# Experts' up stage: GpSimd's remainder pair placed ahead of its fetches, and the second token tile met by the weights' remainder at 128 columns

## The chip, the core and the metric

One Trainium2 chip, one of its cores. The metric is the device time of one launch in microseconds; lower is better. The kernel before took 3091.02 us (median of three runs, 3085.73 to 3091.17).

## What is computed

Two transformer blocks on 256 tokens of width 2048, in float32. The part that matters here is the last stage of the second block, the expert layer (`peer_ffn`). There are 16384 experts; each token chooses 128 of them (8 heads, 16 each) with gates.

```python
def block(args):
    xb, ib, gb = args
    u = expert_down[ib]
    act = jax.nn.gelu(jnp.einsum('tkd,td->tk', u, xb).astype(f32))
    vv = expert_up[ib]
    return jnp.einsum('tk,tkd->td', (gb * act).astype(vv.dtype), vv)
```

The kernel computes it densely for tokens 0 to 191: the activations of all 16384 experts (stage "peer_down"), multiplied with a gate matrix that is zero where an expert was not chosen, and then one dense product with `expert_up` (stage "peer_up", called the up stage here). For tokens 192 to 255 (`QT` = 64 of them) it fetches only the chosen rows of `expert_up` by indirect DMA and VectorE adds them up.

## The kernel before

**Exact products from rounded operands.** TensorE multiplies in the format fp32r. To keep float32 accuracy each operand is split into a rounded part (`hi` for weights, `h` for activations) and a remainder (`lo`, `l`), and three products are summed: rounded with rounded, remainder of the activations with rounded weights, rounded activations with the remainder of the weights.

**Pieces and rounds.** All weights come as one stream of pieces of 128 x 1024 elements, 512 KB each; four pieces are a round. In the up stage (`UPS` = 64 rounds; `UP0` is the number of rounds before it) every engine has its own hand-written program order:

- SyncE (`up_load`, L570) loads a piece into one of eight raw buffers once the remainder of the piece that lay there two rounds before is made (`lo_done`).
- ScalarE (`up_hi`, L1284) rounds piece k of round r into `hi[:, k]` once TensorE is through with piece k of the round before (L1288). For pieces 1 and 3 it also copies the raw piece into two banks of PSUM (`raw_copy`, L1301). Once a round it rounds the activations of the round after next into `hg` (`hidden_hi`, L1266).
- GpSimd makes the remainder of piece 0 of each round, in two halves of 512 columns (`up_lo`, L630, two instructions on L636, called the pair here). It also issues the indirect DMAs: the activations of chosen experts (`fetch_act`, L640, 64 in all, in rounds 1 to 26, five in each of rounds 1 and 2 and two or three after that) and the rows of `expert_up` (`fetch_row`, L646, 128 in all, two or three a round for rounds 3 to 30 and 33 to 62; a fetch moves 512 KB). A row goes into one of five buffers and waits until VectorE has added the row that lay there (L649).
- VectorE makes the remainders of pieces 1, 2 and 3 (`up_lo`, L2296; piece 2 from SBUF, 1 and 3 from the copies in PSUM), adds the fetched rows (`add_row`, L2312), and makes the remainder of the activations (`hidden_lo`, L2249, lines L2253 and L2255; both of its inputs are in SBUF). One round of it is: piece 1, row, piece 2, row, piece 3, perhaps a third row, activations.
- TensorE (`up_piece`, L3013) does per piece and per half of 512 columns five products into two PSUM banks, `a` for tokens 0 to 127 and `b` for tokens 128 to 191. The half's first three use the rounded weights (L3037 to L3039); the other two (L3041, L3042) need the remainder and wait for it (`ready`, L3040). 64 rounds x 4 pieces x 2 halves x 5 are 2560 products; in the last piece of each half of the stage the five stand in another order (L3030, L3031, L2390 to L2392).

**The stationary operands.** `hg` holds, for each slot and piece, 384 columns: remainder of tokens 0 to 127, rounded part of tokens 0 to 127, rounded part of tokens 128 to 191 (64 columns, `h_b`), remainder of tokens 128 to 191 (64 columns). `hl_b` is the last 128 columns, both parts of tokens 128 to 191 beside each other. So L3039 loads 128 columns and writes 128 partitions of `b`, the rounded part's product in the first 64 and the remainder's in the last 64; `add_residual` (L2338) adds the two halves at the end (L2342, L2343). L3041 loads the 64 columns of `h_b` alone and adds into the first 64 partitions.

**Order on GpSimd.** The pair of round 0 stands first. Then come three waits: for the table of rows (`slots_ready`), for the stores of the activations to DRAM (`side_stored`, L657 and L658) and for the end of the stage before (L659). After that the loop of L660 issues in round r the fetches of activations for r, the fetches of rows for r + 1, and then the pair of round r.

Of the kernel before, what the change touches and what calls it, by code (L numbers as in the profile page):

```python
# [29 lines left out]
P = 128  # L30
# [15 lines left out]
NT = 192  # L46
QT = T - NT
# [67 lines left out]
def build(nc, stream, cols, cons, band, dil, x, rpb, w_gates, gains, p_t, w_gd, up_fb,  # L115
          qk_gain, qk_cols, sub_keys, spill, side_acts, out):
    ctx = ExitStack()
    with ctx:
# [7 lines left out]
        def place(name, shape, at, dt=F32):  # L126
            return nc.alloc_sbuf_tensor_at(name, shape, dt, offset=base + at)
# [283 lines left out]
        hg = place("hg", [P, 2, 4, 3 * P], F_AT, F32R)  # L411
# [18 lines left out]
        def raw_up(r, k):  # L430
            return raws[(4 * r + k) % 8]

        def lo_up(k):
            return lo[:, k, :] if k < 2 else lo_x[:, k - 2, :]

        UP0 = ROUND0["peer_up"]
        UPS = 64
# [10 lines left out]
        def acts_at(r):  # L448

            if r < 3:  # L450
                return range(5 * (r - 1), 5 * r)
            return range(10 + (r - 3) * 54 // 24, 10 + (r - 2) * 54 // 24) if r < 27 else range(0)
# [156 lines left out]
        def _(pool):  # L609
# [20 lines left out]
            def up_lo(r):  # L630

                pool.wait_ge(hi_done, (UP0 + r) * 4 + 1)
                for half, used in enumerate((half_used, unit_used)):
                    pool.wait_ge(used, (UP0 + r) * 4 - (3 if r else 1))
                    n = slice(half * NCH, (half + 1) * NCH)
                    nc.gpsimd.tensor_tensor(lo_up(0)[:, n], raw_up(r, 0)[:, n],  # L636
                                            hi[:, 0, n].bitcast(F32), ALU.subtract)\
                        .then_inc(lo_done[0], 1)

            def fetch_act(q):  # L640
                nc.gpsimd.indirect_dma_start(
                    act_q[:, q:q + 1], None, side_acts.rearrange("i j (t a) -> (i j t) a", a=1),
                    bass.IndirectOffsetOnAxis(ap=row_act[:, q:q + 1], axis=0))\
                    .then_inc(got_act[q // 8], 16)
# [8 lines left out]
                    .then_inc(got_row[b], 16)  # L653

            up_lo(0)
            pool.wait_ge(slots_ready, 1)
            for g in range(4):  # L657
                pool.wait_ge(side_stored[g], 16 * 8)  # L658
            pool.wait_ge(unit_used, after("peer_up", 0))  # L659
            for r in range(1, UPS):  # L660
                for q in acts_at(r):
                    fetch_act(q)
                for n in rows_at(r + 1):
                    fetch_row(n)
                up_lo(r)


        @block.scalar
# [1716 lines left out]
        def _(pe):  # L2385
            M = nc.tensor
# [7 lines left out]
            def ready(i, k, half):  # L2394
                pe.wait_ge(lo_done[k], i * 2 + (half + 1))

            def rounded(i, k):
                pe.wait_ge(hi_done, i * 4 + (k + 1))
# [380 lines left out]
            for kb in range(KB):  # L2779
                ins = exact(ps[0:32, 4, 0:T], [m[:, kb, :] for m in (wgd_h, wgd_l)],  # L2780
                            [m[:, kb, :] for m in (xh, xl)], T, kb == 0, kb == KB - 1)
# [199 lines left out]
            for k in range(3):  # L2981
                for tt in range(TT):
                    ins = M.transpose(ps[:, 4 + k, tt * P:(tt + 1) * P],
                                      route[:, k, tt * P:(tt + 1) * P], ident)
# [28 lines left out]
            def up_piece(r, slot, k, half, first=False, last=False):  # L3013

                if k == 0:
                    pe.wait_ge(hl_done, r + 1)
                rounded(r + UP0, k)
                l_a, h_a, h_b, hl_b = (hg[:, slot, k, f] for f in (
                    slice(0, P), slice(P, 2 * P), slice(2 * P, P + NT), slice(2 * P, 3 * P)))
                for n in range(2):  # L3020
                    if first and half == 0:
                        pe.wait_ge(down_summed, 127 + n)
                    elif first and n == 0:
                        pe.wait_ge(acc_read, 1)
                    f = slice(n * NCH, (n + 1) * NCH)
                    w_h, w_l = hi[:, k, f], lo_up(k)[:, f]
                    a, b = (ps[:, 4 * half + 2 * tt + n, :] for tt in range(TT))
                    if last:
                        ready(r + UP0, k, n)
                        M.matmul(b[0:QT], h_b, w_l, start=False, stop=False)  # L3030
                        ins = M.matmul(b, hl_b, w_h, start=False, stop=True)  # L3031
                        if half:
                            ins.then_inc(bank_done, 1)
                        exact(a, (h_a, l_a), (w_h, w_l), NCH, False, True)\
                            .then_inc(bank_done if half else (half_used, unit_used)[n], 1)
                        continue
                    M.matmul(a, h_a, w_h, start=first, stop=False)  # L3037
                    M.matmul(a, l_a, w_h, start=False, stop=False)  # L3038
                    M.matmul(b, hl_b, w_h, start=first, stop=False)  # L3039
                    ready(r + UP0, k, n)  # L3040
                    M.matmul(b[0:QT], h_b, w_l, start=False, stop=False)  # L3041
                    M.matmul(a, h_a, w_l, start=False, stop=False)\  # L3042
                        .then_inc((half_used, unit_used)[n], 1)

# [137 lines left out]
```

## Time and profile before

| | us |
|---|---|
| median of three runs | 3091.02 |
| lowest and highest | 3085.73, 3091.17 |
| the profiled execution | 3095.82 |
| its span from first to last instruction | 3093.5 |
| up stage in it, start of first to start of last but one matmul | 2489.06 to 3087.23 |

| engine | busy us | share of the span |
|---|---|---|
| TensorE matmuls (PE) | 3069.1 | 99% |
| TensorE weight loads (PEld) | 2567.8 | 83% |
| VectorE (DVE) | 1654.9 | 53% |
| ScalarE (ACT) | 1671.4 | 54% |
| GpSimd (POOL) | 2533.4 | 82% |

All times in the profile are from one execution. Matmuls are pipelined, and the end of each is modelled, so the distance from one start to the next tells their pace, and the busy share does not. In the timeline a row has its start, its duration, engine and line, operation, destination and sources, shape and count, and in brackets the idle time before it with what ended it; "128*64" is the size of the stationary operand, 128 rows by 64 columns. "PEclk" is the granted clock of TensorE as a share of 2.4 GHz.

### The profile page before, as it was taken

How to read it: one execution, taken by the hardware profiler on the slowest of the kernel's cores; microseconds unless marked ns; L12 is line 12 of the kernel's file. 1: busy time of each engine (PE TensorE's matmuls, PEld its weight loads, DVE VectorE, ACT ScalarE, POOL GpSimd, SP SyncE). 2: the span in 40 equal slices, each digit the busy share in tenths (PEclk: the TensorE clock that was granted, in tenths of full speed). 3: DMA queues.
4: the chain of work that ended last, by engine and by line, in shares of the span. 5: the costliest groups of instructions: out<-in, count | busy, mean ns of one | idle time of the engine just before them, and what ended most of it. 6: DMA issues, size and time to landing. Idle time of an engine off the chain costs nothing.

```text
span 3093.5 us, 48732 instructions
## 1 busy us (share of the span) xinstructions
PE 3069.1 (99%) x15766; PEld 2567.8 (83%) x15766; DVE 1654.9 (53%) x2846; ACT 1671.4 (54%) x2515; POOL 2533.4 (82%) x1980
## 2 busy tenths in 40 slices
PE   9999999999999999999999999999999999999999
PEld 8888888888888887888888888888888877777777
DVE  5469244434410033655632357167772259998887
ACT  5754543433344455444544434477774467777776
POOL 7888989999999998797788889988889977765553
PEclk9999999999999999999999999999999999999999
DMA  6554655555565565454455655555555589999996
GB/s 237 174 169 152 195 177 184 185 187 183 183 204 194 193 201 176 146 187 164 145 164 189 203 184 189 193 180 175 181 178 195 195 316 355 350 345 355 350 362 239
DMA packets 188519, 659.88 MB, mean 213 GB/s; under 512 B 22864, under 2 KB 28112, under 8 KB 187888
## 3 DMA queue, kind: packets, MB, share of 16 engines
q1 hardware_dynamic: 159168, 573.64, 54.3%
q0 software_dynamic: 20480, 67.15, 6.1%
q10 hardware_dynamic: 8752, 17.60, 1.7%
q8 instruction: 62, 1.02, 0.1%
q14 instruction: 57, 0.47, 0.0%
HBM read 649.92 MB, written 8.39 MB: 213 GB/s over the span
## 4 chain that ended last, share of the span: by engine, by line
PE 94%; DVE 3%; POOL 1%; issue 1%; ACT 0%; DMA 0%; POOLq 0%; DVEq 0%; SPq 0%; ACTq 0%
PE ps L2401 30%; PE ps L2405 15%; PE ps L2499 8%; PE ps L2492 8%; PE ps L2494 8%; PE ps L3037 4%; PE ps L3041 4%; PE ps L3038 4%; PE ps L3042 4%; PE ps L3039 4%; PE ps L2557 3%; POOL lo L620 1%; PE ps L2552 0%; PE ps L2621 0%; DVE pos L2153 0%
## 5 line engine op out<-in xcount | busy, mean ns | idle before, releaser
L620 POOL TENSOR_TENSOR lo<-raw,hi 128x512 fp32r<-128x512 f32 x1656 | 2158.3, 1317 | 326.7 <-PE ps L2405 113.2
L2401 PE MATMUL ps<-xx,hi 128*128 128x512 f32 x4288 | 1521.9, 398 | 5.1 <-DVE xx L1333 5.1
L686 ACT ACTIVATE hi<-raw 128x1024 fp32r<-128x1024 f32 x827 | 869.1, 1059 | 841.6 <-PE ps L2405 432.7
L2405 PE MATMUL ps<-xx,lo 128*128 128x256 f32 x4288 | 1202.4, 280 | 1.7 <-POOL lo L620 1.7
L2401 PEld LDWEIGHTS ps<-xx,hi 128*128 128x128 f32 x4288 | 805.8, 188 | 191.3 <-DVE xx L1333 6.6
L2405 PEld LDWEIGHTS ps<-xx,lo 128*128 128x128 f32 x4288 | 810.4, 189 | 2.8 <-POOL lo L620 2.6
L2492 PE MATMUL ps<-hi,xx 128*128 128x512 f32 x608 | 241.1, 397 | 1.6 <-ACT hi L686 1.1
L2494 PE MATMUL ps<-hi,xx 128*128 128x512 f32 x608 | 237.0, 390 | 0.0
L650 POOL DMA_INDIRECT row<-in_stream,row_up x128 | 134.1, 1048 | 102.2 <-DVE ps L2321 80.9
L3037 PE MATMUL ps<-hi,hg 128*128 128x512 f32 x508 | 201.9, 397 | 0.6 <-issue 0.4
L3038 PE MATMUL ps<-hi,hg 128*128 128x512 f32 x508 | 199.6, 393 | 0.0
L3039 PE MATMUL ps<-hi,hg 128*128 128x512 f32 x508 | 197.7, 389 | 0.0
L2499 PE MATMUL ps<-lo,xx 128*128 128x512 f32 x608 | 188.8, 391 | 2.4 <-POOL lo L620 2.0
L1289 ACT ACTIVATE hi<-raw_up 128x1024 fp32r<-128x1024 f32 x128 | 135.0, 1056 | 80.0 <-PE ps L3042 67.1
L1289 ACT ACTIVATE hi<-raw 128x1024 fp32r<-128x1024 f32 x128 | 134.9, 1056 | 76.5 <-PE ps L3042 68.3
L1678 DVE TENSOR_TENSOR y<-ps,gbc 128x512 f32<-128x512 f32 x16 | 10.3, 686 | 285.2 <-ACT ps L934 285.2
L2321 DVE SCALAR_TENSOR_TENSOR ps<-row,coef,ps 128x1024 f32<-128x1024 f32 x126 | 160.9, 1277 | 0.0
L2229 DVE TENSOR_REDUCE ps<-ps 128x256 f32<-128x512 f32 x80 | 55.9, 699 | 161.2 <-PE ps L2405 161.2
L2499 PEld LDWEIGHTS ps<-lo,xx 128*128 128x128 f32 x608 | 113.3, 188 | 30.0 <-POOL lo L620 6.6
L2494 PE MATMUL ps<-hi,hid_l 128*128 128x512 f32 x352 | 136.9, 389 | 0.0
L2492 PE MATMUL ps<-hi,hid_h 128*128 128x512 f32 x352 | 136.9, 389 | 0.0
L2492 PEld LDWEIGHTS ps<-hi,xx 128*128 128x128 f32 x608 | 114.2, 188 | 27.3 <-issue 2.4
(393 smaller groups left out, 4394.7 us busy)
## 6 DMA issues: line engine op xcount, KB each, us to landing
raw<-in_stream SPq DMA_DIRECT2D x955, 512.0 KB, 3.3
raw_up<-in_stream SPq DMA_DIRECT2D x128, 512.0 KB
side_acts<-side ACTq DMA_DIRECT2D x32, 128.0 KB, 2.3
wg<-in_w_gates ACTq DMA_DIRECT2D x1, 2048.0 KB, 8.8
bias<-in_rpb ACTq DMA_DIRECT2D x1, 2048.0 KB, 8.0
gbc<-in_gains ACTq DMA_DIRECT2D x2, 1024.0 KB, 6.0
spill<-hx ACTq DMA_DIRECT2D x4, 512.0 KB, 3.8
row<-in_stream,row_up POOLq DMA_INDIRECT x128
```

What stands on the lines that cost most here:

```text
L620: nc.gpsimd.tensor_tensor(lo[:, k % 2, n], raw[:, k, n], hi[:, k, n].bitcast(F32), ALU.subtract)\
L686: nc.scalar.activation(hi[:, k, :], raw[:, k, :], ACT.Copy).then_inc(hi_done, 1)
L1289: nc.scalar.activation(hi[:, k, :], raw_up(r, k), ACT.Copy).then_inc(hi_done, 1)
L2321: V.scalar_tensor_tensor(out=accum(n), in0=rows_in[n % 5][:], scalar=c, in1=accum(n), op0=ALU.mult, op1=ALU.add).then_inc(row_used, 1)
L2401: M.matmul(ps[:, b_, :], w_h, xx[:, i_].rearrange("p a t -> p (a t)"), start=first, stop=False)
L2405: return M.matmul(t_bank(b_), w_l, xh[:, i_, :], start=False, stop=last)
L2492: M.matmul(ps[:, 2 * pair + tt, :], ah[:, kb0 + j, t], hi[:, k, f], start=first and j == 0, stop=False)
L2494: M.matmul(ps[:, 2 * pair + tt, :], al[:, kb0 + j, t], hi[:, k, f], start=False, stop=False)
L2499: return M.matmul(ps[:, 2 * pair + tt, :], ah[:, kb0 + j, t], lo[:, k % 2, f], start=False, stop=last and j == 1)
L3037: M.matmul(a, h_a, w_h, start=first, stop=False)
L3038: M.matmul(a, l_a, w_h, start=False, stop=False)
L3039: M.matmul(b, hl_b, w_h, start=first, stop=False)
```

## The change

Two edits. On GpSimd the pair of a round stands one place earlier: rounds 0 and 1 both come ahead of the three waits, and in round r the pair of r + 1 follows the fetches. On TensorE the product of the second token tile with the weights' remainder takes all 128 columns of `hl_b` instead of the 64 of `h_b`, so it also adds remainder times remainder into the last 64 partitions; in the last piece of a half the products with `w_h` and `w_l` change places.

```diff
             up_lo(0)
+            up_lo(1)
             pool.wait_ge(slots_ready, 1)
             for g in range(4):
                 pool.wait_ge(side_stored[g], 16 * 8)
...
                     fetch_act(q)
                 for n in rows_at(r + 1):
                     fetch_row(n)
-                up_lo(r)
+                if r + 1 < UPS:
+                    up_lo(r + 1)
...
-                l_a, h_a, h_b, hl_b = (hg[:, slot, k, f] for f in (
-                    slice(0, P), slice(P, 2 * P), slice(2 * P, P + NT), slice(2 * P, 3 * P)))
+                l_a, h_a, hl_b = (hg[:, slot, k, n * P:(n + 1) * P] for n in range(3))
...
                     if last:
                         ready(r + UP0, k, n)
-                        M.matmul(b[0:QT], h_b, w_l, start=False, stop=False)
-                        ins = M.matmul(b, hl_b, w_h, start=False, stop=True)
+                        M.matmul(b, hl_b, w_h, start=False, stop=False)
+                        ins = M.matmul(b, hl_b, w_l, start=False, stop=True)
...
                     ready(r + UP0, k, n)
-                    M.matmul(b[0:QT], h_b, w_l, start=False, stop=False)
+                    M.matmul(b, hl_b, w_l, start=False, stop=False)
```

## Rows read from the trace of the kernel before

**Rows 1.** The page: its span, and busy time by engine.
```profile
span 3093.5 us, 48732 instructions
...
PE 3069.1 (99%) x15766; PEld 2567.8 (83%) x15766; DVE 1654.9 (53%) x2846; ACT 1671.4 (54%) x2515; POOL 2533.4 (82%) x1980
```

**Rows 2.** Timeline of PE: the up stage, and 5.4 us of the stage "down".
```profile
1000.26 0.39 PE L2492 MATMUL ps<-hi,hid_h 128*128 128x512 f32 x1
...
1005.70 0.39 PE L2492 MATMUL ps<-hi,hid_h 128*128 128x512 f32 x1
...
2489.06 0.39 PE L3037 MATMUL ps<-hi,hg 128*128 128x512 f32 x1
...
2498.72 0.40 PE L3039 MATMUL ps<-hi,hg 128*128 128x512 f32 x1
2503.29 0.69 PE L3041 MATMUL ps<-lo,hg 128*64 128x512 f32 x1 [4.17 <-POOL lo L636]
...
2508.79 0.40 PE L3038 MATMUL ps<-hi,hg 128*128 128x512 f32 x1
...
2633.60 0.47 PE L3037 MATMUL ps<-hi,hg 128*128 128x512 f32 x1
...
2690.46 0.49 PE L3037 MATMUL ps<-hi,hg 128*128 128x512 f32 x1
...
2699.78 0.40 PE L3037 MATMUL ps<-hi,hg 128*128 128x512 f32 x1
...
2709.00 0.40 PE L3037 MATMUL ps<-hi,hg 128*128 128x512 f32 x1
...
3087.23 0.39 PE L2391 MATMUL ps<-lo_x,hg 128*128 128x512 f32 x1
```

**Rows 3.** Windows: stretch, its length, busy by engine, PEclk, DMA share, GB/s.
```profile
2503.30:2508.60 5.30, 5.30 (x13) 3.93 (x14) 2.06 (x2) 1.06 (x1) 4.29 (x4) 0.50 0.66 248
2835.00:2850.00 15.00, 15.00 (x67) 11.52 (x66) 12.44 (x18) 11.21 (x16) 8.50 (x8) 1.00 1.02 403
2577.00:2614.00 37.00, 37.00 (x163) 28.57 (x162) 36.97 (x44) 27.97 (x37) 29.71 (x27) 1.00 0.99 362
```

**Rows 4.** Timeline of POOL: the start of the up stage, and round 16.
```profile
2485.91 2.55 POOL L636 TENSOR_TENSOR lo<-raw,hi 128x512 fp32r<-128x512 f32 x2 [0.50 <-ACT hi L1289]
2495.42 1.10 POOL L641 DMA_INDIRECT act_q<-side_acts,row_act  x1 [6.96 <-DMA side_acts<-side]
...
2500.98 0.95 POOL L641 DMA_INDIRECT act_q<-side_acts,row_act  x1 [0.30 <-issue]
2501.94 2.52 POOL L636 TENSOR_TENSOR lo<-raw_up,hi 128x512 fp32r<-128x512 f32 x2
...
2639.46 2.55 POOL L636 TENSOR_TENSOR lo<-raw,hi 128x512 fp32r<-128x512 f32 x2
```

**Rows 5.** Timeline of ACT: pieces 0 and 3 of round 1.
```profile
2491.65 1.06 ACT L1289 ACTIVATE hi<-raw_up 128x1024 fp32r<-128x1024 f32 x1 [0.27 <-PE ps L3042]
...
2499.95 1.06 ACT L1289 ACTIVATE hi<-raw_up 128x1024 fp32r<-128x1024 f32 x1 [2.67 <-DMA raw_up<-in_stream]
```

**Rows 6.** Groups of PEld, 2630 to 3093 us: line, count, busy, mean ns.
```profile
L3039 PEld LDWEIGHTS ps<-hi,hg 128*128 128x128 f32 x391 | 73.5, 188 | 17.5
...
L3041 PEld LDWEIGHTS ps<-lo,hg 128*64 128x64 f32 x196 | 26.3, 134 | 9.2 <-POOL lo L636 0.8
```

**Rows 7.** Timeline of DVE: round 15, the start of 16, and L2253 in round 22.
```profile
2633.36 1.27 DVE L2309 TENSOR_TENSOR lo<-ps,hi 128x512 fp32r<-128x512 f32 x2
...
2639.34 3.23 DVE L2253 TENSOR_TENSOR hg<-gm,hg 128x512 fp32r<-128x512 f32 x1
...
2642.82 1.27 DVE L2309 TENSOR_TENSOR lo<-ps,hi 128x512 fp32r<-128x512 f32 x2
...
2704.09 0.67 DVE L2253 TENSOR_TENSOR hg<-gm,hg 128x512 fp32r<-128x512 f32 x1
```

**Rows 8.** Waits, 2633 to 2692 us: total us, times, longest.
```profile
POOL row L650 <- DVE ps L2321: 8.8, 8, 1.3
```

## The prediction

> **What bounds it now.** I read the page first: PE is busy 99% of a span of 3093.5 us [rows 1]. A busy PE says little here, so I went to the starts of its matmuls in the timeline [rows 2]. The up stage runs from 2489.06 to 3087.23, which is the last matmul but one; with one more step of 0.23 that is 598.4 us for 2560 matmuls. The reader should see three things in those rows.
>
> First, the pace. From the L3037 at 2699.78 to the one at 2709.00 lies one round, 40 matmuls in 9.22 us, or 230.5 ns each. In the stage "down", where every stationary operand has 128 columns, 24 matmuls of the same moving size take 5.44 us (1000.26 to 1005.70), or 226.7 ns.
>
> Second, a pause at the start: L3039 at 2498.72, and the next matmul at 2503.29, "<-POOL lo L636". After it the granted clock is 0.50 [rows 3], the lower level, 1.2 GHz, and the 13 steps from 2503.29 to 2508.79 take 5.50 us.
>
> Third, six rounds from 2633.60 to 2690.46 take 56.86 us, where six at the pace above take 55.3.
>
> GpSimd's rows [rows 4] show where the pause comes from. The pair of round 0 is done at 2488.46, then GpSimd waits 6.96 us for the store of the activations, issues five fetches from 2495.42 on, and only then makes the pair of round 1, at 2501.94. TensorE sits on that pair. ScalarE had its input, piece 0 of round 1, at 2492.71 [rows 5].
>
> **Part 1, the pair ahead of the fetches, at the start.** With two pairs ahead of the waits, that of round 1 starts at about 2492.8 and ends at 2495.35 (2.55 us, rows 4); TensorE wants it at 2498.95. The pause goes: 4.57 less one normal step of 0.23 is 4.34 us. The low clock goes with it: 5.50 less 13 steps of 0.2305 (3.00) is 2.50 us. Together 6.8 us. Behind the moved pair wait the five fetches, whose own condition ends at about 2495.4 anyway, so they lose nothing.
>
> What is late next? Piece 3 of round 1 is loaded late and rounded from 2499.95 to 2501.01 [rows 5]. Without the pause TensorE comes to it at 2498.25 (start of round 1) plus 3 x 2.3, or 2505.2; that is 4 us of room. Then GpSimd: in the new order it has five fetches (until 2501.9), the pair of round 2 as soon as ScalarE has rounded piece 0 of that round, until 2506.4 (before it ScalarE has the copies of piece 3 and the activations; I put these and the rounding at 2.8 us, a little under three of its instructions of 1.06 [rows 5], so 2503.8), then seven fetches at 1.26 us (2500.98 to the next start, 2501.94, plus the usual gap of 0.3) until 2515.3, and the pair of round 3 with its first half at 2516.6. TensorE wants that at about 2517.2. It fits by half a microsecond. I allow 0.5 us here.
>
> The moved pair also meets VectorE, which is making the remainders of round 0 from SBUF until 2494.4. If the two can't run together, the last of these is done near 2496.8, TensorE wants it at 2497.8; nothing is added.
>
> **Part 2, the pair ahead of the fetches, in the rounds.** In the first half GpSimd waits for VectorE's rows: 8 waits of together 8.8 us in 59 us [rows 8], and its pair waits behind these. So the pair follows VectorE's phase and comes when VectorE is at L2253. That instruction takes 0.67 us alone at 2704.09, and 3.23 us at 2639.34, where the pair runs from 2639.46 to 2642.01 [rows 4, 7]. With it one cycle of VectorE (piece 1 at 2633.36, piece 1 at 2642.82) lasts 9.46 us, longer than TensorE's 9.22, and VectorE has no idle time at all between 2577 and 2614, 36.97 of 37 us [rows 3]. That is the 1.6 us lost between 2633 and 2690: TensorE waits for the activations' remainder.
>
> After the change the row fetches stand behind the pair, some 2.6 us later against VectorE, so their buffers are free and the pair depends on ScalarE's piece 0 alone. It may still overlap L2253, but VectorE then loses only the time for which it would wait for piece 1 anyhow, since the pair no longer moves along with it. I take back the whole 1.6 us. GpSimd itself has 2.56 + 0.3 + 1.26 x 4 or 5, or 7.9 to 9.2 us a round (10.4 twice, at rounds 22 and 26), against a round of 9.07: tight but enough on average, with 4 us between the pair and its use. The rows come 2.6 us later against their use. I allow another 0.5 us for both.
>
> On this collision the Trainium skill ("SBUF — State Buffer", section "Who interferes with whom") says that a VectorE instruction with two SBUF inputs and a GpSimd instruction that reads SBUF exclude each other for a whole instruction. The trace agrees: 3.23 against 0.67 us, held by both halves of the pair.
>
> **Part 3, 128 columns.** No matmul is added; 512 of the 2560 get a stationary operand of 128 columns in place of 64. Its load takes 188 ns in place of 134 [rows 6]. The other 2048 have 188 already and run at the same pace behind one another, so a load of 188 is hidden behind a matmul of 230. The trace of before has no such product in this stage, so I bound it. Lower end of the gain: the pace stays at 230.5, gain 0. Upper end: the pace of "down", 226.7, the only stretch of rows with nothing but 128-column operands and 512-column movers. 598.4 less 6.8 and 1.6 is 590.0 us, or 230.5 a matmul; at 226.7 it would be 580.4, gain 9.6. I take 9.1, nearly that end: the shape of the stage will be that of "down", and only 0.5 us is kept for steps that stay slower after a pause.
>
> For this edit the Trainium skill has a rule that speaks against it ("TensorE: Matmul & The Clock Gate", part 3, the mechanism): a weight load overlaps a running matmul only where their row groups differ, which they don't here. By it the longer load would be paid in full. Rows 6 beside rows 2 speak against it: load plus stream in line would be more than 400 ns, and the pace is 230.5.
>
> **DMA.** Faster rounds want the same bytes in less time: 362 GB/s at a share of 0.99 becomes 362 x 9.2 / 9.07, or 367. Another stretch moved 403 GB/s [rows 3], so I put this at nothing; if that cover is gone, the first half stays at 9.2 us a round, some 3.6 us (28 x 0.13).
>
> **The sum.** 6.8 + 1.6 + 9.1 - 0.5 - 0.5 is 16.5 us off. Profiled execution: 3095.8 to 3079.3 (span 3077.0). Its time stands 4.8 above the median, so the median goes from 3091.0 to **3074.5**.
>
> **Rivals.**
> - *The pace is not from the 64 columns.* The stages differ in other things too (the up stage has VectorE and DMA traffic around it). Then only 8.4 - 1.0 comes: 3083.6. Chance 0.18.
> - *The pause only moves.* The pair of round 3 stands behind seven fetches with half a microsecond of room. If ScalarE is 2 us later than I reckon, TensorE pauses there and may get the low clock again; up to the 6.8 comes back: 3081. For it: the small room. Against: ScalarE was counted with its whole queue, and half a microsecond late costs no more than that. Chance 0.07.
> - *VectorE becomes the bound.* If the pair meets L2253 in each round and the rows come late too, rounds 3 to 30 go at 9.5 us in place of 9.2: 28 x 0.3 is 8 us, which eats parts 1 and 2; with the second half's pace from part 3 (4.5 us) it gives 3087, without it 3091, and with late rows at another 0.25 us a round 3098. For it: VectorE's 36.97 of 37 us. Against: the pair no longer waits for VectorE. Chance 0.10.
> - *The other side: the wide load is not hidden.* Place: L3041, 512 times. Price: 188 - 134 = 54 ns each, 27.6 us, less 7.4 from GpSimd: 3111. It decides from 15 ns of the 54 on (7.4 us over 512). Against it stands rows 6 with the pace. Chance 0.05.
>
> **Chances.** Forecast 0.60, its own range 3070 to 3080. A measurement of this kernel can tell about 0.2%, 6.2 us, so faster means under 3084.8. Faster: 0.60 + 0.12 of the first rival + 0.06 of the second, and 0.01, 0.79. Same: 0.06 + 0.01 + 0.06, 0.13. Slower: 0.03 of the third + 0.05, 0.08. The range runs from 3070 (all of 9.6, and no allowance used) to 3087, which takes in the first two rivals and leaves out most of the last two, some 0.15.
>
> **What would show it.** Right: no POOL wait near 2498 and PEclk 1.00 throughout; L3037 to L3037 over a round 9.07 us; L650 no longer waiting for L2321; the pair starting right behind ScalarE's piece 0; up stage near 582 us. Wrong: a round still at 9.2 (part 3), a wait of TensorE on L636 or for the activations between 2510 and 2780 (part 2), L2253 near 3 us with VectorE full.

## The result, and the profile after

| | before | changed |
|---|---|---|
| median of four runs each, us | 3089.66 | 3071.31 |
| lowest and highest | 3085.73, 3091.17 | 3069.82, 3074.32 |
| the profiled execution | 3095.82 | 3069.82 |
| its span | 3093.5 | 3067.5 |
| up stage: first to last matmul with `hg`, start to start | 2489.06 to 3087.46: 598.4 | 2480.04 to 3061.46: 581.4 |

The changed kernel is faster, with a ratio of 0.9933 (95% interval 0.9911 to 0.9955). The forecast, 3074.5 from 3091.0, is a ratio of 0.9947 and lies in that interval. The two profiled executions differ by much more, 26.0 us of span. The last line of the table divides that: 17.0 us came out of the up stage, and 9.0 us were gone before the up stage began, in code that the change doesn't touch. The forecast had 16.5 for the first and nothing for the second. By itself 17.0 of 3089.66 us would be a ratio of 0.9945.

The page of the changed kernel, with its span, busy time by engine, and two groups of GpSimd (the last column is the idle time before them, and what ended most of it):

```profile
span 3067.5 us, 48732 instructions
...
PE 3046.9 (99%) x15766; PEld 2591.4 (84%) x15766; DVE 1666.6 (54%) x2846; ACT 1671.8 (55%) x2515; POOL 2537.2 (83%) x1980
...
L650 POOL DMA_INDIRECT row<-in_stream,row_up x128 | 130.8, 1022 | 33.9 <-issue 30.6
...
L636 POOL TENSOR_TENSOR lo<-raw_up,hi 128x512 fp32r<-128x512 f32 x64 | 88.9, 1414 | 77.4 <-ACT hi L1291 77.2
```

Beside [rows 1] the number of instructions is the same and TensorE's weight loads take 23.6 us more, since 512 of them are longer. The row fetches, L650, now wait almost only for the issue of the one before, and 1.5 us in the whole stage for VectorE. In the kernel before, their wait was for VectorE, 80.9 us of it:

```profile
L650 POOL DMA_INDIRECT row<-in_stream,row_up x128 | 134.1, 1048 | 102.2 <-DVE ps L2321 80.9
```

The pair, L636, waits for ScalarE alone.

The timeline of PE of the changed kernel, which answers to [rows 2]. The five products stand on L3038 to L3043 here, and L3042 is the one that grew:

```profile
2480.04 0.39 PE L3038 MATMUL ps<-hi,hg 128*128 128x512 f32 x1
...
2516.11 0.39 PE L3043 MATMUL ps<-lo_x,hg 128*128 128x512 f32 x1
2516.91 0.40 PE L3038 MATMUL ps<-hi,hg 128*128 128x512 f32 x1 [0.41 <-DVE hg L2257]
...
2671.08 0.39 PE L3038 MATMUL ps<-hi,hg 128*128 128x512 f32 x1
...
2680.14 0.39 PE L3038 MATMUL ps<-hi,hg 128*128 128x512 f32 x1
...
2780.33 0.39 PE L3040 MATMUL ps<-hi,hg 128*128 128x512 f32 x1
2780.88 0.50 PE L3042 MATMUL ps<-lo,hg 128*128 128x512 f32 x1 [0.17 <-POOL lo L636]
...
3061.46 0.39 PE L2394 MATMUL ps<-hi,hg 128*128 128x512 f32 x1
```

From 2671.08 to 2680.14 lies one round of 40 matmuls in 9.06 us, 226.5 ns each: the pace of the stage "down" in [rows 2], to a fifth of a nanosecond. The pause of 4.34 us (4.57 less a step of 0.23) is gone. The two longest that remain are 0.57 us at 2516.11 (0.80 less a step) and 0.32 us at 2780.33, where the stage changes from its first half to its second. The granted clock stays at 1.00, the level of 2.4 GHz. This is the windows view of the changed kernel, with the columns of [rows 3]:

```profile
2489.00:2500.00 11.00, 11.00 (x50) 9.11 (x49) 5.85 (x10) 8.38 (x12) 9.26 (x9) 1.00 1.01 394
2560.00:2600.00 40.00, 40.00 (x178) 33.14 (x177) 39.93 (x48) 29.98 (x40) 32.71 (x30) 1.00 0.99 369
```

The second line shows VectorE still full, 39.93 of 40 us, and DMA at 369 GB/s, where [rows 3] had 362.

GpSimd's timeline at the start of the changed kernel's up stage, which answers to [rows 4]:

```profile
2476.90 2.55 POOL L636 TENSOR_TENSOR lo<-raw,hi 128x512 fp32r<-128x512 f32 x2 [0.50 <-ACT hi L1291]
2483.76 3.33 POOL L636 TENSOR_TENSOR lo<-raw_up,hi 128x512 fp32r<-128x512 f32 x2 [4.31 <-ACT hi L1291]
2487.25 1.35 POOL L641 DMA_INDIRECT act_q<-side_acts,row_act  x1 [0.17 <-PE ps L3043]
...
2494.09 2.56 POOL L636 TENSOR_TENSOR lo<-raw,hi 128x512 fp32r<-128x512 f32 x2
...
2505.70 2.57 POOL L636 TENSOR_TENSOR lo<-raw_up,hi 128x512 fp32r<-128x512 f32 x2
```

The pair of round 1 starts 3.7 us after the stage does (2483.76 less 2480.04), where it started 12.9 after it before. The four L636 are the pairs of rounds 0, 1, 2 and 3; behind the second stand five fetches, behind the third seven.

### The profile page after: what moved, and what is told of

Its sections match the earlier page's. It is cut to its first block, busy times and chain, and to the rows that moved or that the text cites. A ratio compares the mean times of both kernels' runs of the same rounds, so it can differ in the third digit from the quotient of the medians.

```text
span 3067.5 us, 48732 instructions
## 1 busy us (share of the span) xinstructions
PE 3046.9 (99%) x15766; PEld 2591.4 (84%) x15766; DVE 1666.6 (54%) x2846; ACT 1671.8 (55%) x2515; POOL 2537.2 (83%) x1980
## 4 chain that ended last, share of the span: by engine, by line
PE 94%; DVE 3%; POOL 1%; issue 1%; ACT 0%; DMA 0%; DVEq 0%; POOLq 0%; SPq 0%; ACTq 0%
PE ps L2403 30%; PE ps L2407 16%; PE ps L2501 8%; PE ps L2494 8%; PE ps L2496 8%; PE ps L3042 4%; PE ps L3038 4%; PE ps L3043 4%; PE ps L3039 4%; PE ps L3040 4%; PE ps L2559 3%; POOL lo L620 1%; PE ps L2554 0%; PE ps L2623 0%; DVE pos L2155 0%
## 5 line engine op out<-in xcount | busy, mean ns | idle before, releaser
L620 POOL TENSOR_TENSOR lo<-raw,hi 128x512 fp32r<-128x512 f32 x1656 | 2159.1, 1317 | 316.9 <-PE ps L2407 108.7
L3038 PE MATMUL ps<-hi,hg 128*128 128x512 f32 x508 | 197.8, 389 | 0.4 <-DVE hg L2257 0.4
L3039 PE MATMUL ps<-hi,hg 128*128 128x512 f32 x508 | 197.6, 389 | 0.0
L3040 PE MATMUL ps<-hi,hg 128*128 128x512 f32 x508 | 197.6, 389 | 0.0
L650 POOL DMA_INDIRECT row<-in_stream,row_up x128 | 130.8, 1022 | 33.9 <-issue 30.6
L636 POOL TENSOR_TENSOR lo<-raw_up,hi 128x512 fp32r<-128x512 f32 x64 | 88.9, 1414 | 77.4 <-ACT hi L1291 77.2
L636 POOL TENSOR_TENSOR lo<-raw,hi 128x512 fp32r<-128x512 f32 x64 | 90.9, 1442 | 69.4 <-ACT hi L1291 69.3
```

Source lines behind the costliest of these rows:

```text
L620: nc.gpsimd.tensor_tensor(lo[:, k % 2, n], raw[:, k, n], hi[:, k, n].bitcast(F32), ALU.subtract)\
```

## The experiments

My theory after the result: the three parts of the prediction are real, each independent of the others, and the 9.0 us ahead of the stage are a property of the execution. The rivals: the parts need each other; the pace has another cause than the 64 columns; the time ahead of the stage is the change's. The parts turned out not to be independent.

In all that follows "up stage" is first `hg` matmul to last, start to start, plus one step of 0.23. Each ratio is to runs of the kernel before taken beside that kernel's. Span and up stage are those of the one execution that was profiled.

| kernel | median us (lowest, highest) | ratio to before (95%) | span | up stage starts | up stage |
|---|---|---|---|---|---|
| before, again | 3091.01 (3086.98, 3100.50) | 1.0005 (0.9986 to 1.0024) | 3088.7 | 2483.47 | 599.4 |
| before, a third time | 3088.46 (one run) | | 3086.0 | 2481.71 | 598.5 |
| changed, again | 3074.70 (3071.06, 3083.78) | 0.9958 (0.9943 to 0.9972) | 3068.7 | 2480.93 | 582.0 |
| GpSimd's edit alone | 3084.98 (3078.08, 3093.86) | 0.9985 (0.9972 to 0.9999) | 3087.0 | 2489.66 | 591.6 |
| 128 columns alone | 3086.71 (3081.40, 3094.24) | 0.9981 (0.9968 to 0.9994) | 3088.7 | 2490.06 | 592.9 |
| only round 1's pair ahead | 3084.75 (3080.06, 3092.65) | 0.9989 (0.9978 to 0.9999) | 3078.2 | 2479.66 | 592.7 |
| that pair behind the waits | 3074.07 (3072.28, 3076.05) | 0.9940 (0.9921 to 0.9958) | 3074.2 | 2485.03 | 583.3 |
| the two hl_b products apart | 3073.72 (3071.74, 3075.70) | 0.9947 (0.9928 to 0.9966) | 3073.5 | 2485.52 | 582.2 |
| two products of five at 64 | 3081.53 (3077.61, 3088.17) | 0.9972 (0.9958 to 0.9985) | 3081.2 | 2487.01 | 588.4 |
| one at 96 | 3086.16 (3079.20, 3095.26) | 0.9989 (0.9976 to 1.0002) | 3084.5 | 2486.15 | 592.6 |
| all five at 64 | 3081.13 (3077.67, 3089.90) | 0.9976 (0.9962 to 0.9990) | 3077.0 | 2481.49 | 589.7 |

A single kernel's runs spread over up to 16 us, while three profiles of the kernel before give the up stage as 598.6, 599.4 and 598.5, and two of the changed kernel as 581.6 and 582.0. So the up stage's length is what I read the experiments by; a difference under a microsecond says nothing in it.

### Each edit alone

GpSimd's new order, with the fourth product at 64 columns:

```diff
-                l_a, h_a, hl_b = (hg[:, slot, k, n * P:(n + 1) * P] for n in range(3))
+                l_a, h_a, h_b, hl_b = (hg[:, slot, k, f] for f in (
+                    slice(0, P), slice(P, 2 * P), slice(2 * P, P + NT), slice(2 * P, 3 * P)))
...
-                    M.matmul(b, hl_b, w_l, start=False, stop=False)
+                    M.matmul(b[0:QT], h_b, w_l, start=False, stop=False)
```

> The GpSimd edit alone, the stationary operand of L3041 still 64 columns. Theory (the two edits act apart): no pause near the start of the up stage and no loss near round 15 to 21, but rounds of 9.17 to 9.23 us as before; up stage 598.6 - 6.8 - 1.6 = 590.2 us, about 8.4 us faster than before. Rival (the quicker rounds of the changed kernel come from GpSimd's order, through fewer collisions): rounds of 9.07 us here too, up stage near 582.

Measured: 591.6, with no pause near round 1, and a single one of 0.68 us at 2526 for the activations' remainder. The step in the later rounds is unchanged. The edit saves 7.1 of the forecast 8.4. Half of what is missing is that wait. The other half shows in the starts of the rounds, here that of round 3 in the kernel before:

```profile
2523.52 0.40 PE L3037 MATMUL ps<-hi,hg 128*128 128x512 f32 x1
```

From it to 2633.60 [rows 2] the kernel before ran twelve rounds in 110.08 us, 9.17 each, at the same granted clock of 1.00. With GpSimd's edit alone the same twelve take 110.70 us (2527.25 to 2637.95), 9.23 each, which is 0.6 us more. Of the other two profiles of the kernel before one has 9.17 in these rounds and one has 9.23. So one mixture of widths has two paces. I don't know what selects them.

The wide operand alone, with GpSimd in its old order:

```diff
-            up_lo(1)
...
-                if r + 1 < UPS:
-                    up_lo(r + 1)
+                up_lo(r)
```

> The 128 columns alone, GpSimd in its old order. Theory: undisturbed rounds take 9.07 us, but the pause at the start stays (6.8 us) and in the first half VectorE, tied to GpSimd's pair, needs 9.46 to 9.65 us a round, so that the quicker pace is lost again as waits of TensorE for the activations' remainder between rounds 7 and 22: up stage 591 to 593 rather than the 589.5 of plain subtraction. Rival (width has no part in the pace): 598 to 599.

Measured: 592.9, so it saves 5.7. Two things take from the gain. Here are the timeline of PE and the waits of 2520 to 2690 us in this kernel (engine, line, what it waited for; total us, times, longest):

```profile
2504.87 0.80 PE L3040 MATMUL ps<-lo,hg 128*128 128x512 f32 x1 [4.86 <-POOL lo L636]
...
2561.18 0.39 PE L3036 MATMUL ps<-hi,hg 128*128 128x512 f32 x1
...
2701.39 0.39 PE L3036 MATMUL ps<-hi,hg 128*128 128x512 f32 x1
```

```profile
POOL row L650 <- DVE ps L2321: 16.4, 17, 1.3
...
PE ps L3036 <- DVE hg L2255: 1.1, 3, 0.4
```

The first is the old pause. TensorE waits 4.86 us for the pair where it waited 4.17 before, since it arrives sooner. The others are the rounds: GpSimd's fetches wait for VectorE 17 times, and TensorE in its turn waits for VectorE's remainder of the activations. The two starts of rounds above show the price: rounds 7 to 21 take 140.2 us, where fifteen at 9.07 are 136.0. That is 4.2 us lost, where the kernel before lost 1.6. Some 3.4 of it stand at the step to the first product of a round, the one that waits for that remainder; the waits view names only 1.1 us of them. The windows view has 173 matmuls in the 40 us from 2560, where the changed kernel has 178.

So the edits are not independent: 7.1 and 5.7 are 12.8, and together they give 17.0. A round of 9.07 us is shorter than VectorE's cycle of 9.46 while that is coupled to GpSimd [rows 7]. The wide operand pays in the first half of the stage only once the pair no longer waits behind VectorE's rows. The other 4.2 us belong to the two together. (That this equals the loss above is chance. Most of it can be named: 2.6 us more lost in these rounds than before, 0.7 us of a longer pause, and the 0.6 us of the twelve rounds with GpSimd's edit alone.)

### The fetches or the waits ahead of the pair

Only round 1's pair is moved; later ones stand behind the fetches as before:

```diff
-                if r + 1 < UPS:
-                    up_lo(r + 1)
+                if r > 1:
+                    up_lo(r)
```

> The changed kernel, but only the pair of round 1 stands ahead; from round 2 on the pair is behind the fetches as before. Theory: the pause of round 1 is gone, but round 2's pair now stands behind twelve fetches (five of round 1, five and two of round 2, 15 us) and comes late by some us, and GpSimd waits for VectorE's rows again with VectorE near 9.5 us a round: up stage 586 to 592. Rival (all of the GpSimd gain is the pause at the start): 582 to 583.

Measured: 592.7, a little above the range that I gave. GpSimd's timeline and PE's in this kernel:

```profile
2483.38 3.31 POOL L636 TENSOR_TENSOR lo<-raw_up,hi 128x512 fp32r<-128x512 f32 x2 [4.33 <-ACT hi L1291]
2486.87 1.35 POOL L641 DMA_INDIRECT act_q<-side_acts,row_act  x1 [0.17 <-PE ps L3043]
...
2501.83 0.97 POOL L650 DMA_INDIRECT row<-in_stream,row_up  x1 [0.30 <-issue]
2502.84 2.49 POOL L636 TENSOR_TENSOR lo<-raw,hi 128x512 fp32r<-128x512 f32 x2
```

```profile
2504.16 0.79 PE L3042 MATMUL ps<-lo,hg 128*128 128x512 f32 x1 [5.48 <-POOL lo L636]
```

Now the twelve fetches of rounds 1 and 2 stand in one row. It is 16.0 us from 2486.87 to the pair of round 2 at 2502.84, and TensorE waits 5.48 us for that pair. The pause has moved one round on. In the changed kernel the pair of round 2 stands between them, at 2494.09. It is the shift in every round that takes the pause away, not the first pair alone.

Round 1's pair behind the three waits, but ahead of the fetches:

```diff
             up_lo(0)
-            up_lo(1)
...
             pool.wait_ge(unit_used, after("peer_up", 0))
+            up_lo(1)
```

> The changed kernel, but the pair of round 1 stands behind the three waits and ahead of the five fetches. Theory (it is the fetches, not the waits, that made it late): the pair runs from about 2494.5 to 2497.1 by the clock of the profile before, 4.5 us ahead of its old place, and TensorE wants it at 2498.9; no pause, up stage within 1 us of the changed kernel's 581.6; the five fetches start 2.6 us later, so round 3's pair may be late by up to 2.6 us. Rival (the store of the activations is what it hangs on): a pause of 1 us or more in round 1.

Measured: 583.3, 1.7 above the first profile of the changed kernel and 1.3 above the second, which is more than the 1 us that I gave. GpSimd's and PE's timelines:

```profile
2491.27 2.55 POOL L636 TENSOR_TENSOR lo<-raw_up,hi 128x512 fp32r<-128x512 f32 x2 [6.94 <-ACT hi L1291]
...
2512.00 2.54 POOL L636 TENSOR_TENSOR lo<-raw_up,hi 128x512 fp32r<-128x512 f32 x2
```

```profile
2513.35 0.50 PE L3042 MATMUL ps<-lo,hg 128*128 128x512 f32 x1 [0.20 <-POOL lo L636]
...
2523.55 0.39 PE L3038 MATMUL ps<-hi,hg 128*128 128x512 f32 x1 [1.44 <-ACT hi L1291]
```

The pair starts 6.2 us into the stage and TensorE doesn't wait for it in round 1. So the pause of the kernel before was due to the five fetches, not to the waits. Round 3's pair starts 27.0 us into the stage (2512.00 less 2485.03) and 25.7 in the changed kernel, so it is 1.3 us later, and TensorE waits for it at 2513.35. That costs 0.36 us (0.59 from the start before to this one, less a step): the room in the changed kernel was about a microsecond, not the half that I reckoned. The second row is a wait for ScalarE's rounding of 1.6 us some ten microseconds on. ScalarE's own waits just before it are for VectorE's remainders, 1.70 us at 2515.33 and 0.91 at 2520.11. Between the two kernels only GpSimd's place for that pair differs; how that reaches VectorE and ScalarE I didn't trace. Neither brings a low clock; a window of this kernel from 2523:

```profile
2523.40:2530.00 6.60, 6.45 (x29) 5.45 (x30) 5.72 (x8) 4.39 (x6) 5.67 (x6) 1.00 0.98 374
```

### What sets the pace

The forecast took nearly the pace of "down" once all operands were 128 wide. It came, but why it does is another question. My theories were that each 64-column product costs a fixed time, and then that the mixture of widths does; a rival was that two products in a row with the same operand run faster. Each kernel has GpSimd's new order.

The same operand no longer twice in a row:

```diff
-                    M.matmul(a, l_a, w_h, start=False, stop=False)
                     M.matmul(b, hl_b, w_h, start=first, stop=False)
+                    M.matmul(a, l_a, w_h, start=False, stop=False)
```

> The changed kernel with L3040 and l_a's product in exchanged places, so that the stationary operand hl_b is no longer loaded twice in a row. Theory (the width sets the pace): 226.7 ns a matmul, rounds of 9.07, up stage 581 to 583. Rival (the pace comes from the same operand standing twice in a row): 230 ns or more, up stage 590.

Two of the five at 64 columns:

```diff
-                    M.matmul(a, l_a, w_h, start=False, stop=False)
+                    M.matmul(a[0:64], l_a[:, 0:64], w_h, start=False, stop=False)
...
-                    M.matmul(b, hl_b, w_l, start=False, stop=False)
+                    M.matmul(b[0:64], hg[:, slot, k, 2 * P:2 * P + 64], w_l, start=False, stop=False)
```

> GpSimd in the new order, L3042 back at 64 columns and the product of l_a with the rounded weights at 64 columns too (it leaves out the activations' remainder for tokens 64 to 127). The suspected cost doubled. Theory (each narrow load costs about 20 ns): a group of five takes 1173 ns, 234.6 a matmul, up stage about 600. Rival (only a change of pattern matters, not the number): 1147 to 1153 as before, up stage 590. Second rival (narrow loads are cheaper in themselves): under 1133.

One at 96:

```diff
-                    M.matmul(b, hl_b, w_l, start=False, stop=False)
+                    M.matmul(b[0:96], hg[:, slot, k, 2 * P:2 * P + 96], w_l, start=False, stop=False)
```

> The changed kernel with 96 of the 128 columns of hl_b in L3042 (it leaves out remainder times remainder for tokens 160 to 191). Theory (any width other than the neighbours' breaks the pace): 229 to 231 ns a matmul, up stage 588 to 590. Rival (it is the 64, half the array or less): 226.7 and 582.

All five at 64:

```diff
+                    full = P if first else 64
-                    M.matmul(a, h_a, w_h, start=first, stop=False)
-                    M.matmul(a, l_a, w_h, start=False, stop=False)
-                    M.matmul(b, hl_b, w_h, start=first, stop=False)
+                    M.matmul(a[0:full], h_a[:, 0:full], w_h, start=first, stop=False)
+                    M.matmul(a[0:64], l_a[:, 0:64], w_h, start=False, stop=False)
+                    M.matmul(b[0:full], hl_b[:, 0:full], w_h, start=first, stop=False)
...
-                    M.matmul(b, hl_b, w_l, start=False, stop=False)
-                    M.matmul(a, h_a, w_l, start=False, stop=False)\
+                    M.matmul(b[0:64], hl_b[:, 0:64], w_l, start=False, stop=False)
+                    M.matmul(a[0:64], h_a[:, 0:64], w_l, start=False, stop=False)\
```

> The changed kernel with all five products of a group at 64 columns (it leaves out tokens 64 to 127 and the activations' remainder of tokens 128 to 191, except in the first and last group of each half). Theory (it is the mixture of widths that breaks the pace, since two narrow of five cost 13 ns a group and one 20): 226.7 ns a matmul, up stage about 581. Rival (each narrow operand costs something in itself, some 6 ns): 230 or more, up stage 590. Second rival (narrow operands alone are faster, their load being 134 rather than 188 ns): under 225, up stage under 577.

All are read from the same 200 us of the second half, in the windows view, where TensorE has no wait. The first count is TensorE's matmuls. A matmul is shown 0.39 us long at steps of 0.23, so some two of the count began before the stretch, and the step is 200 us over the count less 2. (From start to start over whole rounds it comes out within 0.1 ns of that, 226.7 for the changed kernel.) First the kernel with GpSimd's edit alone (one product of five at 64), then the changed kernel, the one with products apart, two at 64, one at 96, and all five at 64:

```profile
2820.00:3020.00 200.00, 200.00 (x869) 153.51 (x868) 165.57 (x222) 149.95 (x197) 104.02 (x90) 1.00 0.97 362
```

```profile
2820.00:3020.00 200.00, 200.00 (x884) 165.58 (x884) 181.45 (x227) 152.66 (x199) 110.61 (x91) 1.00 0.97 363
```

```profile
2820.00:3020.00 200.00, 200.00 (x884) 165.68 (x883) 181.45 (x226) 152.71 (x200) 112.14 (x93) 1.00 0.97 366
```

```profile
2820.00:3020.00 200.00, 200.00 (x874) 145.02 (x873) 164.58 (x221) 150.85 (x197) 105.56 (x91) 1.00 0.96 363
```

```profile
2820.00:3020.00 200.00, 200.00 (x867) 157.88 (x866) 163.79 (x220) 150.10 (x196) 103.56 (x90) 1.00 0.96 360
```

```profile
2820.00:3020.00 200.00, 200.00 (x871) 116.65 (x870) 166.11 (x223) 150.50 (x197) 104.09 (x90) 1.00 0.96 360
```

By the rule above the steps are 230.7, 226.8, 226.8, 229.4, 231.2 and 230.1 ns. What follows:
- Repeating an operand does nothing: 226.8 with the two apart.
- The fixed price per narrow product falls: one costs 3.9 ns a step, two only 2.6. The up stage of 588.4 is near the rival (590), not the theory (600).
- The mixture falls as the only cause: with all five at 64 columns there is none, and the step is 230.1, as the first rival had it.
- Less loading doesn't help: the weight loads are busy 116.65 of 200 us there, 165.58 in the changed kernel, and the changed kernel is the faster one.
- 96 columns are no better than 64; the up stage, 592.6, is even above the 588 to 590 of the theory.

What holds over all kernels run is only this: every kernel whose products all have 128 columns runs the second half at 226.7, and every kernel with a narrower one at 229.4 to 231.2 (and the kernel before once at 229.3, in rounds 3 to 14). So the 64 columns are shown to cost the pace; the mechanism stays open. I tried no 128-column operand with half of its columns zero, and no 32.

### The two kernels again

The changed kernel and the kernel before, unchanged, to see what repeats:

> The changed kernel once more. Theory (the 9.0 us that its profile saved ahead of the up stage come from a pace of the stage ffn that differs from one execution to the next, 352.5 or 346.0 ns for a pair of matmuls, whatever the kernel): over the runs the times spread by several us, and a profile may show either pace; the difference to before is that of the up stage, 17 us, a ratio of 0.9945. Rival (the change reaches back into ffn): the profile shows 346.0 again in this kernel, never in one with the old up stage, and the ratio is 0.9915.

> The kernel before once more, for its profile. Theory (the pace of stage ffn differs from execution to execution): the up stage takes 598 to 599 us again, while what lies ahead of it is anything from 2479 to 2491 us; a pace of 346 in ffn for the kernel before would settle it. Rival (the pace ahead of the up stage belongs to the kernel): 2489 us and 352.5 again.

> A third profile of the kernel before, with the same expectations: up stage 598 to 599 us; ffn at 346 or 352.5 by the theory, at 352.5 by the rival.

Measured: the up stage repeats within 1 us, the time ahead of it doesn't, and the ratio of the changed kernel is 0.9958. The tile view of hid_h, the hidden activations of "down", gives the first and last start of that stage, in the kernel before as profiled first, in the changed kernel, and in the kernel before as profiled again (count, then shortest, median and longest in ns, then the two starts):

```profile
L2492 PE MATMUL ps<-hi,hid_h x352: 389/389/395, 876.5 to 1115.2; 128*128 128x512 f32 x176
```

```profile
L2494 PE MATMUL ps<-hi,hid_h x352: 389/389/397, 867.6 to 1106.4; 128*128 128x512 f32 x176
```

```profile
L2492 PE MATMUL ps<-hi,hid_h x352: 389/389/397, 867.5 to 1106.3; 128*128 128x512 f32 x176
```

"Down" takes 238.7 or 238.8 us in all three. It begins at 876.5 in one execution of the kernel before and at 867.5 in another: the 8.9 us by which the changed kernel was ahead there are not the change's. The stretch from 500 to 800 us, first kernel before, then changed, then before again, shows how it goes:

```profile
500.00:800.00 300.00, 300.00 (x1703) 258.93 (x1702) 123.08 (x159) 118.78 (x133) 272.83 (x212) 1.00 0.55 184
```

```profile
500.00:800.00 300.00, 300.00 (x1736) 263.14 (x1735) 123.95 (x162) 122.03 (x135) 278.24 (x216) 1.00 0.56 188
```

```profile
500.00:800.00 300.00, 300.00 (x1736) 263.14 (x1735) 123.84 (x162) 121.94 (x135) 278.13 (x216) 1.00 0.56 188
```

The same instructions run at 1703 or at 1736 matmuls in 300 us, with the granted clock at 1.00 and TensorE busy throughout in both. The first profile of before and the kernels with one edit alone had the lower number, all others the higher.

A second stretch, later on, has two paces too, and not in step with the first. The 170 us from 2300, in the changed kernel and in the kernel before as profiled again:

```profile
2300.00:2470.00 170.00, 170.00 (x984) 149.86 (x983) 44.10 (x85) 73.48 (x127) 155.24 (x124) 1.00 0.59 194
```

```profile
2300.00:2470.00 170.00, 170.00 (x965) 147.39 (x964) 43.31 (x84) 73.44 (x127) 151.71 (x121) 1.00 0.58 191
```

All thirteen profiles have 984 to 986 or 965 to 966 here. The kernel before had 985 in its first profile, which was the slow one at 500 us, and 965 in the other two. So each stretch has its pace by itself, and neither goes with the kernel.

## Why the prediction was right, and where not

**Part 1, pause and low clock (6.8 us).** Right. No wait for L636 in round 1, and the clock stays at 1.00 in the window from 2489. GpSimd's plan holds almost to the number: shifted by the 9.0 us by which the stage starts sooner, I had the seven fetches end at 2506.3, and round 3's pair starts at 2505.70, without a wait of TensorE. Some luck is in that. The five fetches were not to lose anything by standing behind the moved pair, but it ended at 2487.09, and they ended at 2494.0 in place of 2492.9; and round 2's pair, for which I had counted a wait for ScalarE, had none and came 0.7 us sooner than planned. The kernel with that pair 1.3 us later, which waits 0.36 for it, shows that the room was about a microsecond. The step about which I said "nothing is added", the moved pair against VectorE's remainders of round 0, shows in VectorE's timeline of the changed kernel:

```profile
2482.93 4.71 DVE L2311 TENSOR_TENSOR lo_x<-raw,hi 128x512 fp32r<-128x512 f32 x4
```

Four of these take 4.71 us, where two take 1.28 elsewhere (2509.80 below), so about 2.2 us were lost; GpSimd's pair took 3.33 in place of 2.55 at the same time. Both were held, and TensorE waited for neither. The Trainium skill ("SBUF — State Buffer", section "Who interferes with whom") has a VectorE instruction with two SBUF inputs and a GpSimd instruction that reads SBUF lock each other out whole; these two numbers agree with it, in that both engines lost time while they overlapped.

**The two allowances (0.5 each).** The first was put at round 3's pair. The pause came one round later and from another engine. VectorE's timeline of the changed kernel:

```profile
2505.02 0.17 DVE L2330 TENSOR_TENSOR coef<-act_q,gate_q 128x8 f32<-128x8 f32 x1 [2.65 <-DMA act_q<-side_acts,row_act]
...
2508.61 1.29 DVE L2319 TENSOR_SCALAR ps<-row,coef 128x1024 f32<-128x1024 f32 x1 [2.10 <-DMA row<-in_stream,row_up]
2509.80 1.28 DVE L2311 TENSOR_TENSOR lo_x<-raw_up,hi 128x512 fp32r<-128x512 f32 x2
...
2513.40 2.88 DVE L2255 TENSOR_TENSOR hg<-gm,hg 128x512 fp32r<-128x512 f32 x1
2516.20 0.41 DVE L2257 TENSOR_TENSOR hg<-gm,hg 128x256 fp32r<-128x256 f32 x1
```

VectorE waits 2.65 us for the fetched activations and 2.10 us for the first row, then L2255 meets the next pair and takes 2.88 us in place of 0.67. So L2257 ends at 2516.6, and TensorE has waited for it since 2516.34: the 0.57 us above. In the second profile of the changed kernel the same wait was 0.90 us. The prediction named such an effect ("The rows come later against their use"), but only a part of this one is it. The first row's fetch in the kernel before:

```profile
2511.16 0.95 POOL L650 DMA_INDIRECT row<-in_stream,row_up  x1 [0.30 <-issue]
```

Counted from the start of the stage it was issued at 22.1 us there and at 23.5 in the changed kernel (2503.49), 1.4 us later. VectorE used it at 33.0 there (2522.08) and would have at 26.5 here (2508.61 less 2.10), 6.5 us sooner. The larger part is that the pause, which had given the fetch its time, is gone.

**Part 2, the rounds (1.6 us).** Right in kind. The waits view of the changed kernel, 2617 to 2676 us, against [rows 8]:

```profile
POOL lo L636 <- ACT hi L1291: 3.2, 4, 1.2
```

No row waits for VectorE there. The collision itself did not go, as the prediction allowed. This is the activations' remainder (L2253 before, L2255 after) in the tile view, first before, then changed, with shortest, median and longest in ns:

```profile
L2253 DVE TENSOR_TENSOR hg<-gm,hg x64: 672/680/3234, 2407.5 to 3073.7; 128x512 fp32r<-128x512 f32 x64
```

```profile
L2255 DVE TENSOR_TENSOR hg<-gm,hg x64: 676/1343/3537, 2398.5 to 3048.1; 128x512 fp32r<-128x512 f32 x64
```

It is held in more rounds than before (a median of 1343 for 680), and VectorE is as full. But the pair no longer moves along with VectorE, and the rounds run at 9.07 us. What I did not see is that this part is worth more beside part 3 than alone: 1.6 us at the old pace, 4.2 at the new one, as the kernel with 128 columns alone shows. The cause of the 1.6 us was read from VectorE's rows, and the waits view of the kernel before names no such wait of TensorE. But its timeline bears it out: 1.3 us stand at the step to the first product of a round, as at 2643.22, which comes 0.3 us after the end of the remainder (L2255, 2642.49 for 0.41). At 2516.91 in the changed kernel it is 0.3 us too.

**Part 3, the pace (9.1 of at most 9.6).** Right in kind, and a little too small. From the kernel with GpSimd's edit alone, 591.6, to the changed kernel, 581.6 or 582.0, are 9.6 to 10.0 us. The pace before was read from one round at 2699.78, and 598.4 was divided by 2560 though it holds 2559 steps; in the second half of the stage the step was 230.7, a little above the 230.5 of the forecast. At a step of 226.7 ns 2559 steps are 580.1 us; the up stage takes 581.4, start to start. The remaining 1.3 us is 0.57 at 2516 and some 0.6 about 2780, where one half of the stage follows the other and TensorE waits in short pieces for remainders, as the row at 2780.88 shows. Loads of 188 ns go with steps of 226.7, so one behind the other they would leave 39 ns for a matmul. The rival "the wide load is not hidden" fell with that. The Trainium skill has a rule ("TensorE: Matmul & The Clock Gate", part 3, "The mechanism") that a weight load overlaps a matmul only where their row groups differ. It does not hold here by itself; the same section excepts a load into a background weight buffer, which no row here shows. The same page, section "Back-to-back issue gap", gives 216 ns from one isolated matmul of this size to the next and 131 ns in a sustained stream with weight loads; no run here shows either, and the fastest stream of this size that was read is at 226.7.

**DMA at nothing.** Right: 369 GB/s where I reckoned 367, and no wait for a piece of the stream among TensorE's. VectorE's two waits for fetched data, before 2505.02 and 2508.61, are not in that figure; they reached TensorE as the 0.57 us above.

**The sum.** 16.5 forecast, 17.0 measured in the up stage, and 3071.31 lies in the range. That the sum comes so near is in part two errors that cancel: parts 1 and 2 less the allowances were 7.4 forecast and 7.1 measured, part 3 was 9.1 forecast and 9.6 to 10.0 measured. By the ratio 0.9933 on the 3089.66 of the same comparison the changed kernel stands at 3069.0, a microsecond under the range's low end; on 3091.02 it is 3070.3. The second comparison, 0.9958, is 13.0 us off, and the forecast's 0.9947 lies in both intervals, as does the 0.9945 that the up stage gives by itself. So the first comparison went some 3.7 us beyond what the change did (20.7 less 17.0), and the second 4 us short of it.

**The step that failed** is in "Chances": the range "runs from 3070 (all of 9.6, and no allowance used)". It is made of the terms of the change alone. That puts the rest of the kernel at nothing: it takes it to repeat from one execution to the next, as does the sentence that carries the profiled execution's 4.8 us above the median over to the changed kernel. It doesn't: 9 us come or go with the pace of the stretch before "down", a few more with that of the stretch from 2300, the changed kernel's profiled execution stood 1.5 below its own median and not 4.8 above, and the interval of the ratio is 6.8 us wide to each side of its middle (0.0022 of 3091). An end on the low side needed some of those microseconds too. Of the terms of the change the most mis-sized is part 3, whose upper end of 9.6 was reached or passed by 0.4 us. None of the rivals came true.

## What to carry to other kernels

Where an in-order engine both computes for TensorE and issues fetches, put the computing one step ahead in every round: here, moving the first alone only moved the pause. An edit of TensorE's pace pays only as far as the engine next in line can follow, so price such edits together and look at the cycle of that engine against the new round. And read a change of half a per cent in its own stage, not in the span: here the rest of the kernel moves by half as much as the change by itself.

## What the runs showed of the hardware that was not expected

- Identical instructions of the stretch ahead of "down" run at two paces, 1703 or 1736 matmuls in 300 us, at the same granted clock. It is worth 8.9 us by the start of "down". The stretch from 2300 has two as well, 965 or 984 in 170 us, and which one it has doesn't follow from the first. What selects them was not found.
- The up stage of the kernel before shows two paces as well, 9.17 or 9.23 us a round in rounds 3 to 14, at the same granted clock; two of its three profiles have the first there, and all have the second from round 22 to the end of the half.
- With one, two or all five stationary operands of 64 columns, or one of 96, the mean step in the second half is 229.4 to 231.2 ns; with all at 128 it is 226.7, with the same moving size. All at 64 are nearly as slow as one in five. So a narrower operand, with a shorter load, saves nothing here and costs up to 2%.
- Pauses of 0.57 us (changed kernel), 0.36 and 1.6 us (pair behind the waits) brought no low clock; those of 4.34 us (before), 5.02 us (128 columns alone) and 5.65 us (only round 1's pair ahead) were followed by the level of 1.2 GHz. All are from start to start, less a step.
